# Old keys in units of four pages: 128x2048 VectorE instructions in place of 128x1024

## The chip, the cores and the metric

The kernel runs on one core of a Trainium2 chip. The metric is the time of one execution on the device in microseconds (us); lower is better. The profile is of one execution on that core.

## What is computed

One inference step of a two-layer decoder trunk, for a prompt of 1024 tokens and for 8 samples of one new token each, whose past is 8192 positions long. Layer 0 runs stick-breaking attention beside an RWKV-7 recurrence, layer 1 a gated DeltaNet; each is followed by a convolutional feed-forward network. All is fp32. What matters here is the attention of the samples over their old keys and values, which lie in a pool of pages of 128 positions:

```python
rows = pool[layer, page_table]                       # 64 pages of (128, 8 heads, 64) per sample
z = einsum('bthd,bshd->bhts', q, past_k) * scale + bias
u = log_sigmoid(-z);  after = reverse_cumsum(u) - u
w = exp(log_sigmoid(z) + after)
o = einsum('bhts,bshd->bthd', w, past_v)
```

Per sample that is 64 key pages and 64 value pages of 256 KB each; for 8 samples 512 of each.

## The kernel before, in words

The program is a row of phases with a barrier between them: projections of layer 0 (queries and keys, values, then the RWKV columns in `pb_phase`), prompt attention, the recurrent stage (`rwkv_phase`), output projection, feed-forward, and then layer 1. TensorE has all the projections. The old pages are read beside two of the phases, and the class `Pages` holds their buffers, semaphores and steps.

**A page.** SyncE loads key pages (`load_key_page`, L1019 to L1024): it waits until the slot is free (semaphore `k_used`), reads the page's number from the table, and issues one DMA of 256 KB into a ring of 8 slots (`RING`). The DMAs of a slot count on the slot's own semaphore `k_in`. GpSimd does the same for value pages (`load_values`, L1078), into a ring of their own.

**A unit of keys.** `keys_dve` (L1108 to L1122) waits for its pages, multiplies them with the sample's query, which lies broadcast over all partitions in `pg_q` (L1117, result in `pg_prod`), which frees the slots through `k_used`; then it waits for that multiply and sums over the 64 elements of each head (L1121, result in `pg_z`). The next multiply waits for that sum through `reduced`, since there is one `pg_prod`. A unit is two pages, 128x1024 elements.

**The query.** `load_q` (L1017) loads a sample's query when all 64 pages of the sample before are multiplied. In SyncE's queue it stands behind the first eight key pages of the sample (`load_keys`, L1026 to L1032).

**pb_phase** (L843 to L961) does 14 tiles of 128 columns with two buffers. The pages of sample 0 go along. VectorE's order in a tile: take the rounding rest of the next tile's weights (`rest_weights`, L254), two units of keys (four in each of the last two tiles, which are written out behind the loop), then mix the tile's row with the row before it (L934 to L937), which frees the weight buffer. SyncE's order: weights of an even tile, eight key pages, weights of an odd tile. The weights' DMA waits for the mixing of the tile two before.

**rwkv_phase** (L1367 to L2147) has nine iterations by hand, i = 0 to 8. Iteration i solves chunk pair i of the prompt (two chunks of 64 tokens; `level`, a triangular inverse by doubling, L2010 to L2018), walks the state through pair i - 1 (`state`, L2022 to L2030), prepares pair i + 1 (`gate_ones`, `tanh`, `keys`, `lora_bias`, `sigmoid_ones`, `log_decays`, `modified_keys`, `products`, `bonus`), reads the old values of sample i on TensorE (`values_pe`, L1056), and multiplies the old keys of sample i + 1 on VectorE. The order on VectorE is written out: between the other steps stand calls `more(n)`, each of which takes n units from the sample's list, and `more(NPG)` at the end of the iteration takes what is left. The calls from one bias to the next are: 2 units after `bias_dve`; then softplus, `blocks_t`, `exponents_dve`, `state`, `blocks`; then 1, 1, 1 (after blocks, masked keys, gate), tanh, keys, level 1, then 1, lora bias, 1, `state`, sigmoid, 1, level 2, 2, log decays, 1, centre, 1, level 3, 2, modified keys, 1, normed, 2, level 4, 1, products, 2, outputs, bonus, 2, level 5, and the last 10. In all 32 units, of which 22 before level 5.

The next iteration begins with `bias_dve` (L1130), which needs all 64 pages' scores. From it follow ScalarE's logarithms, the softplus, TensorE's cumulative sums (L1045, L1046), the exponents and the weights `pg_w`, and after these TensorE may begin with the sample's value pages.

Of the kernel before, what the change touches and what calls it, by code (L numbers as in the profile page):

```python
# [17 lines left out]
ALU = mybir.AluOpType  # L18
# [3 lines left out]
P = 128  # L22
# [820 lines left out]
def pb_phase(T):  # L843
# [11 lines left out]
    with ExitStack() as ctx:  # L855
# [61 lines left out]
        def _(dve):  # L917
# [8 lines left out]
            def tile(i, st, j, last=False):  # L926
                if not last:
                    rest(2 * i + j + 1, 1 - j)

                first, units = (RING // 2 * j, RING // 4) if i is not LAST else (0, RING // 2)  # L930
                for n in range(units):
                    pages.keys_dve(dve, 0, i if i is not LAST else LAST + j, first + 2 * n)
                dve.wait_ge(row_in, 6 * i + 3 * j + 3 + 6)
# [32 lines left out]
class Pages:  # L966
# [10 lines left out]
    def __init__(self, T, ctx):  # L977
# [15 lines left out]
        self.qr = self.fold[0:NS, :]  # L993
        self.prod = sb("_prod", [P, 2, D_A])
        self.z = sb("_z", [P, H_A, NPG])
# [112 lines left out]
    def keys_dve(self, dve, b, m, n):  # L1108

        g = self.RING * m + n  # L1110
        if not isinstance(g, int) or g == 0:
            dve.wait_ge(self.q_in, 16 * b + 16)
        for e in range(2):
            dve.wait_ge(self.k_in[n + e], 16 * self.loads * b + 16 * m + 16)

        dve.wait_ge(self.reduced, NPG // 2 * b + self.RING // 2 * m + n // 2 + 1)
        dve.tensor_tensor(self.prod[:, :, :], self.kp[:, n:n + 2, :], self.q[:, :].unsqueeze(1).to_broadcast([P, 2, D_A]),  # L1117
                          ALU.mult).then_inc(self.k_used, 2)
        dve.wait_ge(self.k_used, self.RING + NPG * b + g + 2)
        z = self.z[:, :, g:g + 2] if isinstance(g, int) else self.z[:, :, bass.ds(g, 2)]  # L1120
        dve.tensor_reduce(z.rearrange("p h n -> p n h"), self.prod[:, :, :].rearrange("p n (h d) -> p n h d", h=H_A),  # L1121
                          AX.X, ALU.add).then_inc(self.reduced, 1)  # L1122
# [5 lines left out]
    def bias_dve(self, dve, b):  # L1128
        dve.wait_ge(self.reduced, NPG // 2 * b + NPG // 2 + 1)
        dve.tensor_tensor(self.zb[:, :].rearrange("p (h n) -> p h n", h=H_A), self.z[:, :, :],  # L1130
# [236 lines left out]
def rwkv_phase(T):  # L1367
# [17 lines left out]
    with ExitStack() as ctx:  # L1385
# [526 lines left out]
        def _(dve):  # L1912
# [151 lines left out]
            for i in range(NPAIR + 1):  # L2064
                local, walk, sample = i < NPAIR, i >= 1, i < NS
                units = iter(range(0, NPG, 2))

                def more(n):
                    for _, g in zip(range(n if i + 1 < NS else 0), units):
                        pages.keys_dve(dve, i + 1, g // Pages.RING, g % Pages.RING)  # L2070

# [972 lines left out]
```

## Time and profile before

| | |
|---|---|
| Median of 3 runs | 4905.45 us (4897.6 to 4918.18) |
| The profiled execution's time | 4911.91 us |
| Its span in the profile | 4909.5 us |
| Mean granted TensorE clock | 0.887 |
| PE, DVE, ACT, POOL busy | 4047.4, 2406.4, 1128.4, 384.7 us |
| `pb_phase` | about 245 to 450 us |
| `rwkv_phase` | about 736 to 1830 us; keys until 1628 |
| DVE multiplies of keys (L1117) | x256, 313.2 us busy |
| DVE sums of keys (L1121) | x256, 312.7 us busy |

The profile gives for each engine its busy time, for each instruction its start and length, for each idle time of an engine what ended it, and for each DMA its issue and the time to its landing. PE is TensorE, DVE is VectorE, ACT is ScalarE, POOL is GpSimd, SPq is the queue of SyncE, which issues the key pages' DMAs. A time such as 1096.13 is us from the span's start. Where a helper records the instructions of many steps they have one line: L1914 is such a helper. Engines run their own streams and meet only at semaphores, so a share of busy time alone doesn't say what ends a stage.

### The profile page before, as it was taken

What the parts mean: (1) busy time and instruction counts of PE and PEld (TensorE: products, weight loads), DVE (VectorE), ACT (ScalarE), POOL (GpSimd) and SP (SyncE); (2) the same over time, 40 slices, a digit from 0 to 9 for tenths busy, and PEclk for the clock granted to TensorE, in tenths of its full rate; (3) what the DMA queues carried; (4) which work ended last, traced back from release to release, by engine and by line L of the source; (5) the groups of instructions that cost most, each with busy time, mean ns of one, the idle gap of its engine ahead of it and who ended that gap; (6) DMA issues with size and microseconds to landing.
All of it is one profiled execution on the core that took longest, in us unless ns stands there. A gap on an engine that the chain in (4) does not pass through costs nothing. (4 is left out here: it accounts for less than half of the span.)

```text
span 4909.5 us, 79431 instructions
## 1 busy us (share of the span) xinstructions
PE 4047.4 (82%) x29645; PEld 3363.8 (69%) x29645; DVE 2406.4 (49%) x3151; ACT 1128.4 (23%) x1776; POOL 384.7 (8%) x709
## 2 busy tenths in 40 slices
PE   6786887777777758899989699969899456999999
PEld 6685323333333437899989698857777356999999
DVE  2156878888888432444431244444444343334411
ACT  3211552212122111222220222232222112222300
POOL 0000003222222200000000000000000000000000
PEclk8898998888888859999999899987777578999999
DMA  2153007878788513111112222220110132111122
GB/s 95 69 157 121 26 26 280 280 271 275 272 277 275 180 49 116 52 43 52 43 62 77 86 79 87 86 67 18 36 36 6 46 121 78 46 49 43 47 78 65
DMA packets 214323, 512.08 MB, mean 104 GB/s; under 512 B 32305, under 2 KB 69569, under 8 KB 207546
## 3 DMA queue, kind: packets, MB, share of 16 engines
q1 hardware_dynamic: 155914, 321.58, 20.2%
q0 software_dynamic: 58192, 187.57, 10.7%
q8 instruction: 141, 2.31, 0.2%
q14 instruction: 76, 0.62, 0.0%
HBM read 454.87 MB, written 54.56 MB: 104 GB/s over the span
## 5 line engine op out<-in xcount | busy, mean ns | idle before, releaser
L262 PE MATMUL ps<-ffn_hh,up_wh 128*128 128x344 f32 x2112 | 678.4, 321 | 60.0 <-DVE up_wl L254 60.0
L264 PE MATMUL ps<-ffn_hl,up_wh 128*128 128x344 f32 x2112 | 676.7, 320 | 0.0
L263 PE MATMUL ps<-ffn_hh,up_wl 128*128 128x344 f32 x2112 | 676.0, 320 | 0.0
L262 PEld LDWEIGHTS ps<-ffn_hh,up_wh 128*128 128x128 f32 x2112 | 398.6, 189 | 61.0 <-issue 61.0
L1056 PE MATMUL ps<-pg_v,pg_w 128*8 128x512 f32 x1024 | 343.4, 606 | 78.9 <-DMA pg_v<-in_v_pages 76.3
L263 PEld LDWEIGHTS ps<-ffn_hh,up_wl 128*128 128x128 f32 x2112 | 398.6, 189 | 0.0
L264 PEld LDWEIGHTS ps<-ffn_hl,up_wh 128*128 128x128 f32 x2112 | 398.5, 189 | 0.0
L457 PE MATMUL ps<-down_ah,down_wh 128*128 128x344 f32 x1056 | 343.0, 325 | 31.9 <-DVE down_al L491 18.9
L1117 DVE TENSOR_TENSOR pg_prod<-pg_k,pg_q 128x1024 f32<-128x1024 f32 x256 | 313.2, 1224 | 71.7 <-DMA pg_q<-scratch_pg_q 25.5
L458 PE MATMUL ps<-down_ah,down_wl 128*128 128x344 f32 x1056 | 339.9, 322 | 0.0
L459 PE MATMUL ps<-down_al,down_wh 128*128 128x344 f32 x1056 | 339.9, 322 | 0.0
L1078 POOL DMA_DIRECT2D pg_v<-in_v_pages x512 | 277.3, 542 | 665.5 <-PE ps L1056 451.6
L1121 DVE TENSOR_REDUCE pg_z<-pg_prod 128x16 f32<-128x1024 f32 (+1 forms) x256 | 312.7, 1221 | 11.4 <-DVE pg_prod L1117 0.2
L262 PE MATMUL ps<-hh,odd_wh 128*128 128x344 f32 x792 | 258.3, 326 | 63.4 <-DVE odd_wl L254 63.4
L1056 PEld LDWEIGHTS ps<-pg_v,pg_w 128*8 128x8 f32 x1024 | 43.0, 98 | 328.6 <-DMA pg_v<-in_v_pages 299.1
L264 PE MATMUL ps<-hl,odd_wh 128*128 128x344 f32 x792 | 254.8, 322 | 0.0
L263 PE MATMUL ps<-hh,odd_wl 128*128 128x344 f32 x792 | 254.7, 322 | 0.0
L457 PEld LDWEIGHTS ps<-down_ah,down_wh 128*128 128x128 f32 x1056 | 200.6, 190 | 36.5 <-issue 30.1
L458 PEld LDWEIGHTS ps<-down_ah,down_wl 128*128 128x128 f32 x1056 | 201.4, 191 | 0.0
L459 PEld LDWEIGHTS ps<-down_al,down_wh 128*128 128x128 f32 x1056 | 200.7, 190 | 0.0
L262 PEld LDWEIGHTS ps<-hh,odd_wh 128*128 128x128 f32 x792 | 150.4, 190 | 72.0 <-ACT odd_row L2207 41.8
L254 DVE TENSOR_TENSOR down_wl<-down_w,down_wh 128x896 fp32r<-128x896 f32 (+1 forms) x48 | 54.4, 1136 | 280.8 <-ACT down_wh L249 280.8
(410 smaller groups left out, 7368.0 us busy)
## 6 DMA issues: line engine op xcount, KB each, us to landing
pg_k<-in_k_pages SPq DMA_DIRECT2D x512, 256.0 KB, 4.8
pg_v<-in_v_pages POOLq DMA_DIRECT2D x512, 256.0 KB, 5.0
up_w<-in_w_ff SPq DMA_DIRECT2D x44, 1034.0 KB, 4.8
odd_w<-in_w_odd SPq DMA_DIRECT2D x33, 526.0 KB, 4.0
scratch_odd_rows<-odd_cv POOLq DMA_DIRECT2D x32, 516.0 KB, 4.5
down_w<-in_w_down SPq DMA_DIRECT2D x32, 448.0 KB, 3.4
dn_x<-scratch_odd_rows SPq DMA_DIRECT2D x8, 1536.0 KB, 8.2
scratch_x<-out_x POOLq DMA_DIRECT2D x16, 516.0 KB, 3.0
```

What stands on the lines that cost most here:

```text
L254: dve.tensor_tensor(lo, w, hi.bitcast(F32), ALU.subtract).then_inc(rest_ready, 1)
L262: pe.matmul(out, wh, xh, start=(k == 0), stop=False)
L263: pe.matmul(out, wl, xh, start=False, stop=False)
L264: mm = pe.matmul(out, wh, xl, start=False, stop=(k == n - 1))
L457: pe.matmul(out, hi, ah[:, k, g[c]], start=(k == 0), stop=False)
L458: pe.matmul(out, lo, ah[:, k, g[c]], start=False, stop=False)
L459: mm = pe.matmul(out, hi, al[k][:, g[c]], start=False, stop=(k == FT - 1))
L1056: pe.matmul(self.T.ps[c:c + H_A, 7, :], wts[:, :, g], self.vp[:, n, :], start=(g < 4), stop=(g >= NPG - 4), tile_position=(0, c), skip_gro ...
L1078: pool.dma_start(self.vp[:, g % self.RING, :], self.T.io["v_pages"][bass.ds(page, 1), :, :] .rearrange("a p n -> (a p) n")).then_inc(self. ...
L1117: dve.tensor_tensor(self.prod[:, :, :], self.kp[:, n:n + 2, :], self.q[:, :].unsqueeze(1).to_broadcast([P, 2, D_A]), ALU.mult).then_inc(se ...
L1121: dve.tensor_reduce(z.rearrange("p h n -> p n h"), self.prod[:, :, :].rearrange("p n (h d) -> p n h d", h=H_A), AX.X, ALU.add).then_inc(se ...
```

## The change

A unit becomes four pages. `keys_dve` waits for four slots' DMAs, multiplies 128x2048 elements in one instruction, frees four slots with it, and sums 128x2048 elements in the next. `pg_prod` has four page places in place of two. The counts on `reduced` follow. In the tile loop of `pb_phase` there is one unit where there were two (two where there were four at the end). In `rwkv_phase` `more(n)` still counts in steps of two pages: it raises a target by 2n pages and issues a unit whenever four pages are due. So the units stand after `bias_dve` (4 pages due), after the masked keys (8), level 1 (12), the sigmoid (16), level 2 (20), centre (24), after level 3 (28), normed (34, unit 28 to 31), level 4 (36), products (40), bonus (44), and five at the end. The ring keeps its eight slots, and the loads and their order stay as they are.

```diff
@@ pb_phase, VectorE
-                first, units = (RING // 2 * j, RING // 4) if i is not LAST else (0, RING // 2)
+                first, units = (RING // 2 * j, RING // 8) if i is not LAST else (0, RING // 4)
                 for n in range(units):
-                    pages.keys_dve(dve, 0, i if i is not LAST else LAST + j, first + 2 * n)
+                    pages.keys_dve(dve, 0, i if i is not LAST else LAST + j, first + 4 * n)
@@ Pages.__init__
-        self.prod = sb("_prod", [P, 2, D_A])
+        self.prod = sb("_prod", [P, 4, D_A])
@@ Pages.keys_dve
-        for e in range(2):
+        for e in range(4):
             dve.wait_ge(self.k_in[n + e], 16 * self.loads * b + 16 * m + 16)
 
-        dve.wait_ge(self.reduced, NPG // 2 * b + self.RING // 2 * m + n // 2 + 1)
-        dve.tensor_tensor(self.prod[:, :, :], self.kp[:, n:n + 2, :], self.q[:, :].unsqueeze(1).to_broadcast([P, 2, D_A]),
-                          ALU.mult).then_inc(self.k_used, 2)
-        dve.wait_ge(self.k_used, self.RING + NPG * b + g + 2)
-        z = self.z[:, :, g:g + 2] if isinstance(g, int) else self.z[:, :, bass.ds(g, 2)]
+        dve.wait_ge(self.reduced, NPG // 4 * b + self.RING // 4 * m + n // 4 + 1)
+        dve.tensor_tensor(self.prod[:, :, :], self.kp[:, n:n + 4, :], self.q[:, :].unsqueeze(1).to_broadcast([P, 4, D_A]),
+                          ALU.mult).then_inc(self.k_used, 4)
+        dve.wait_ge(self.k_used, self.RING + NPG * b + g + 4)
+        z = self.z[:, :, g:g + 4] if isinstance(g, int) else self.z[:, :, bass.ds(g, 4)]
@@ Pages.bias_dve
-        dve.wait_ge(self.reduced, NPG // 2 * b + NPG // 2 + 1)
+        dve.wait_ge(self.reduced, NPG // 4 * b + NPG // 4 + 1)
@@ rwkv_phase, VectorE
-                units = iter(range(0, NPG, 2))
+                at = [0, 0]
 
                 def more(n):
-                    for _, g in zip(range(n if i + 1 < NS else 0), units):
-                        pages.keys_dve(dve, i + 1, g // Pages.RING, g % Pages.RING)
+                    at[1] = min(at[1] + 2 * n, NPG)
+                    while i + 1 < NS and at[0] + 4 <= at[1]:
+                        pages.keys_dve(dve, i + 1, at[0] // Pages.RING, at[0] % Pages.RING)
+                        at[0] += 4
```

## Rows read from the trace of the kernel before

**Rows 1.** Busy time by stretch, recurrent stage: stretch, length, engines, clock, DMA share, GB/s
```profile
1108.00:1236.00 128.00, 97.30 (x1007) 49.35 (x1006) 111.14 (x116) 27.04 (x51) 36.59 (x66) 0.86 0.82 279
```

**Rows 2.** Waits of VectorE, 736 to 1632 us: total us, times, longest
```profile
DVE pg_prod L1117 <- DMA pg_q<-scratch_pg_q: 25.5, 6, 4.4
...
DVE pg_prod L1117 <- DMA pg_k<-in_k_pages: 2.0, 3, 1.3
```

**Rows 3.** Waits of TensorE, 736 to 1632 us
```profile
PE ps L1574 <- ACT rw_mr L1802: 89.6, 7, 16.3
```

**Rows 4.** Timeline of VectorE, one sample: start, length, instruction, idle before
```profile
995.67 0.69 DVE L1130 TENSOR_TENSOR pg_zb<-pg_z,vecs_sb 128x512 f32<-128x512 f32 x1
...
1024.08 0.36 DVE L1919 TENSOR_SCALAR rw_eg<-rw_eg 128x256 f32<-128x256 f32 x1
...
1035.81 0.87 DVE L1914 TENSOR_TENSOR rw_dh<-rw_Hx,ps 64x256 f32<-64x256 f32 x2 [0.16 <-PE ps L1596]
...
1056.17 0.72 DVE L2014 COPY_PREDICATED rw_mxm<-consts,ps 128x512 f32<-128x512 int32 x1
...
1096.13 1.23 DVE L1117 TENSOR_TENSOR pg_prod<-pg_k,pg_q 128x1024 f32<-128x1024 f32 x1 [0.31 <-DVE rw_mxt L2017]
1097.39 1.22 DVE L1121 TENSOR_REDUCE pg_z<-pg_prod 128x16 f32<-128x1024 f32 x1
...
1119.66 1.22 DVE L1117 TENSOR_TENSOR pg_prod<-pg_k,pg_q 128x1024 f32<-128x1024 f32 x1
...
1122.17 0.69 DVE L1130 TENSOR_TENSOR pg_zb<-pg_z,vecs_sb 128x512 f32<-128x512 f32 x1
```

**Rows 5.** Timeline of SyncE's queue: first start, length until the last's end
```profile
1098.18 25.14 SPq L1023 DMA_DIRECT2D pg_k<-in_k_pages  x20
1123.50 0.33 SPq L1017 DMA_DIRECT2D pg_q<-scratch_pg_q  x1
...
1102.02 2.17 SPq L1023 DMA_DIRECT2D pg_k<-in_k_pages  x2
```

**Rows 6.** Waits of SyncE's queue, 1095 to 1124 us
```profile
SPq L1022 <- DVE pg_prod L1117: 1.1, 2, 1.0
```

**Rows 7.** Timeline of VectorE in the projection stage, one tile
```profile
326.00 1.22 DVE L1117 TENSOR_TENSOR pg_prod<-pg_k,pg_q 128x1024 f32<-128x1024 f32 x1
...
331.20 1.22 DVE L934 TENSOR_TENSOR pb_xs<-pb_row 128x1024 f32<-128x1024 f32 x1
...
332.53 1.29 DVE L937 SCALAR_TENSOR_TENSOR pb_xs<-pb_xs,pb_w,pb_row 128x1032 f32<-128x1032 f32 x1
339.34 1.23 DVE L254 TENSOR_TENSOR pb_wl<-pb_w,pb_wh 128x1024 fp32r<-128x1024 f32 x1 [5.52 <-ACT pb_wh L249]
```

**Rows 8.** Waits of TensorE, 245 to 430 us
```profile
PE ps L262 <- DVE pb_wl L254: 28.1, 12, 4.0
```

**Rows 9.** Instructions of the tile pg_k: ns min/median/max, first and last start
```profile
L1117 DVE TENSOR_TENSOR pg_prod<-pg_k,pg_q x256: 1204/1225/1236, 250.8 to 1625.4; 128x1024 f32<-128x1024 f32 x128
L1914 DVE TENSOR_TENSOR pg_k<-pg_k,rw_kv x3: 2291/2292/2293, 1783.1 to 1800.6; 128x2048 f32<-128x2048 f32 x3
...
L2134 DVE TENSOR_REDUCE rw_sa<-pg_k x1: 3569/3569/3569, 1785.4 to 1785.4; 128x32 f32<-128x2048 f32 x1
```

**Rows 10.** Timeline of ScalarE, 1021 to 1026 us
```profile
1025.14 0.29 ACT L1743 ACTIVATE rw_sg<-rw_eg 128x128 f32<-128x128 f32 x1
```

**Rows 11.** Timeline of TensorE: the last products before level 3
```profile
1052.85 1.10 PE L1537 MATMUL ps<-rw_mxt,rw_my 64*64 64x64 f32 x32
```

**Rows 12.** Timeline of GpSimd: one value page
```profile
1085.61 0.54 POOL L1078 DMA_DIRECT2D pg_v<-in_v_pages  x1 [0.62 <-issue]
```

**Rows 13.** DMA issues, KB each, median us to landing: 1085:1125, 1100:1110, 1112:1124
```profile
pg_k<-in_k_pages SPq DMA_DIRECT2D x27, 256.0 KB, 5.3
...
pg_k<-in_k_pages SPq DMA_DIRECT2D x7, 256.0 KB, 6.1
...
pg_k<-in_k_pages SPq DMA_DIRECT2D x9, 256.0 KB, 3.4
```

## The prediction

> **What bounds the kernel now.** The change touches old keys alone, so I read first where those 512 pages are multiplied: in the stage that projects the RWKV columns (245 to 450 us; 64 pages, sample 0) and in the recurrent stage (736 to 1632 us; 448 pages, samples 1 to 7). A "unit" is one multiply and its sum.
>
> The busy times by stretch say that in the recurrent stage VectorE is the busiest engine, with 111.1 of 128 us in a stretch of one sample's length, while the DMA engines stand at 0.82 and move 279 GB/s [rows 1]. The reader should see two things near a limit, not one. The waits say what VectorE stops for: 4.2 us a sample for the query's DMA (25.5 in six times), key pages hardly ever (2.0 us in all) [rows 2]; the rest of its idle time is in gaps between dependent instructions and waits under 3 us. TensorE waits 89.6 us for a ScalarE copy, behind VectorE's work [rows 3]: TensorE has room. So a sample takes what VectorE's instructions take plus the query wait: bias at 995.67, bias again at 1122.17, period 126.5 us [rows 4]. In the last 26 us of it, from 1096.13, ten units stand back to back, 2.61 us apart (nine steps in 23.53 us) [rows 4].
>
> Then the queue that feeds them. In that same tail SyncE issues 20 key pages in 25.14 us, 1.26 us each, and waits 1.1 us for free slots in all [rows 5, 6]: VectorE takes a page per 1.31 us, SyncE can issue one per 1.26. The key stream is as close to its limit as VectorE. This is what the sum hangs on.
>
> In the projection stage VectorE's timeline shows a loop of 14.5 us a tile: two units (from 326.00), three mixing instructions (331.20 to 332.53 + 1.29), 5.5 us idle for the next tile's rounded weights, their split (339.34, some 1.15 us until the next unit), again [rows 7]. The weights' DMA waits for that mixing. TensorE waits for the split 28.1 us in 12 times, 2.3 us each [rows 8]. So here the units lie on the path.
>
> **What one unit costs.** A 128x2048 multiply stands in the trace at 2.292 us, one of 128x1024 at 1.225 us [rows 9]: 0.158 us saved where two become one. A contiguous sum over 128x2048 isn't there. The 128x1024 one takes 1.22 us, as its multiply does, so I take 1.22 + (2.292 - 1.225) = 2.29 us; bounds: that, and twice 1.22 = 2.44 us. (The 3.57 us of the 128x2048 sum in rows 9 reads across rows of the tile; this one reads along them as before, so it isn't a bound.) With the gaps of 0.03 and 0.14 us of rows 4, a unit of four pages steps 2.29 + 0.03 + 2.29 + 0.14 = 4.75 us against 2 x 2.61 = 5.23: 0.48 us saved. There are 16 such per sample: 7.7 us a sample, 54 us for seven. If that were all, the answer would be easy; the parts follow.
>
> **Part 1, projection stage.** From the first unit's start to the mixing's first subtraction is 5.20 us (326.00 to 331.20) [rows 7]; with one unit 2.29 + 0.14 + 2.22 = 4.65. Saved 0.55 us on the loop in 12 tiles = 6.6 us, and in the last two tiles (four units each, two after) 0.95 us each = 1.9. SyncE: all four slots of a half are now freed at once, 2.3 us after the unit's start; its four issues at 1.26 us end 2.3 + 4 x 1.26 = 7.3 us after it, or 7.8 with a turn of its loop, and the mixing ends 4.65 + 2.6 = 7.3 us after it, so the odd tile's weights, which stand behind those issues, may leave up to 0.5 us late. I keep 8.5 us of gain; bounds 0 and 8.5. TensorE's slack of 2.3 us covers 0.55.
>
> **Part 2, recurrent stage, per sample, from bias to bias.**
> (a) The first four pages: one unit for two, -0.5 us, in front of everything.
> (b) From there to the second state update. Units now start only when four pages are due: none before the masked keys, none between the gate's "plus one" and the tanh. VectorE then meets waits that units covered: the tanh needs ScalarE's result, 1.35 us after the gate's instruction began (1024.08, then 1025.14 + 0.29) [rows 4, 10]; and the state update already waits for TensorE, 0.16 us at 1035.81 [rows 4]. It cannot start earlier, since TensorE's part follows the start of the stretch and not the units. VectorE arrives there 1.5 to 2 us early and idles. It has done 12 pages there instead of 14. The saving in this stretch is lost and two pages are postponed.
> (c) From there to the last level of the solve: 15 units before (15 x 2.48 + 5 x 0.14 = 37.9 us), 8 after (8 x 4.61 = 36.9), and two gaps of some 0.15 us fewer: -1.2 us. The levels before have slack: TensorE ends level 3 at 1053.95, VectorE takes it at 1056.17 [rows 4, 11]. The value pages, which TensorE takes in between, come as before: GpSimd issues one per 1.16 us, by its own pace (0.54 us and 0.62 of issue) [rows 12].
> (d) The tail: five units for ten. Before 26.04 us (1096.13 to 1122.17). VectorE alone needs 5 x 4.61 + 4 x 0.14 = 23.6. But the ring has eight pages, so now it is two halves, each freed at once when a multiply ends, and reloaded by four issues in a row. From the end of a multiply the first issue takes 0.8 us (1096.13 + 1.23 to 1098.18), three more take 3.8, the loop's turn 0.5 for one half (two issues over it span 2.17, so 2.17 - 0.33 = 1.84 apart instead of 1.26) [rows 4, 5]: the last page is issued 4.6 to 5.0 us later and lands after L. VectorE is back at that half 2.29 + 0.17 + 4.75 = 7.2 us after the multiply's end. It waits when L is over about 2.4 us. L is 5.3 us (median of this stretch), 6.1 at its fullest, 3.4 once the values have stopped [rows 13]. Walking the five units with 5.3 for the first two reloads and 3.4 for the rest, from the first unit's start: starts at 0, 7.0 (waited 2.3), 12.2 (0.4), 17.7 (0.8), 22.5 (0), end 27.1. That is +1.1 us against 26.04, not -2.4. With one L throughout the tail takes about 18.4 + 2L.
> (e) The query: its DMA stands behind the eight pages of the next sample, of which the last multiply now frees four, not two. Before: multiply ends 1119.66 + 1.22, query issued 1123.50, 2.6 us [rows 4, 5]; now 0.8 + 4 x 1.26 = 5.1 with the issue. That is 2.5 later; the last sum is 1.07 us longer; so the wait at the query grows by 1.4 us, six times.
> Sum: 7 x (-0.5 - 1.2 + 1.1) + 6 x 1.4 = -4.2 + 8.4 = +4.2 us. With part 1: -4.3 us. Six semaphore counts change and cost nothing. The product buffer grows by 4 KB per partition and moves no work.
>
> The profiled execution took 4911.9 us (span 4909.5), which gives 4907.6; it lies 6.5 above the median, so for the median 4905.45 I forecast 4901.
>
> **The tiling rule.** The rows give each VectorE instruction a fixed part of 0.158 us whatever its size [rows 9]. The Trainium skill ("VectorE: DVE Perf Modes", the section on the TRN2 errata) says that one large tile pays the latency once and many small ones pay it each time, so tile large. By that alone this change gains everything; that is the first rival. **The landing.** A page takes 3.4 us to land in the quiet and 5.3 beside the values [rows 13]. The Trainium skill ("DMA: Bandwidth & Descriptors", the cost table after the chain of events) gives 2.0 us plus bytes over 436 GB/s, 2.6 us for a page: by it the tail would take 23.6 us and the time would be some 25 us lower; the trace disagrees.
>
> **Rivals.**
> A. All of VectorE's saving arrives: 54 + 8.5 = 62 us, 4843. For it: the tail is pure VectorE. Against: SyncE idles 1.1 us in 25. Chance 0.07.
> B. Pages land at 3 us in the tail, and the tail falls to 18.4 + 6 = 24.4 us: (-1.7 - 1.6) x 7 + 8.4 - 8.5 = -23; with the query hardly later, 4875 to 4882. For it: bursts are further apart. Against: the DMA engines are full there. 0.12.
> C. The projection stage gives nothing, since the burst of key issues holds its weights back: 4910. 0.15.
> D. Slower: the half ring starves VectorE in the tail because four pages at a time land later than single pairs. Price: at L = 7 the tail takes 32.4 us, +6.3 per sample, 7 x 4.6 + 8.4 - 8.5 = +32, 4937. It decides from L = 6.5 on. For it: 6.1 already occurs. Against: as many bytes in more time. 0.10.
> E. The change does less than it says: if the wide sum costs 2.44 us, 16 x 0.15 x 7 = 17 us come back where VectorE isn't waiting: 4918 at most. 0.06.
> The forecast itself has 0.50. A measurement of this kernel tells 0.5%, 24.5 us, from no change. Faster by more: A, most of B: 0.17. Slower: D, 0.10. Same: 0.73. The range reaches from rival B to just short of D, with E and C inside: 4875 to 4928.
>
> **What would show it.** 128 multiplies of 128x2048 near 2.29 us and 128 sums near 2.29; VectorE busy time lower by 128 x 0.31 = 40 us; waits for key pages in the recurrent stage up from 2.0 to some 25 us; the query wait from 25.5 to some 34; the wait at 1035.81 from 0.2 to some 1.5 us a sample, and a new one at the tanh; a period near 126.5 us; a loop of 13.9 us in the projection stage. Wrong: if the key waits stay near 2 us, the ring's argument falls, and the time goes to B; if the period passes 130 us, to D.

## The result, and the profile after

The changed kernel takes 4932.29 us (median of 5 runs, 4920.85 to 4948.9) against 4905.45: the ratio is 1.0058, interval 1.0034 to 1.0083. It is slower by 27 us. The forecast was 4901 and the range ended at 4928, so both missed; the side was that of rival D, to which the prediction gave 0.10.

The arithmetic went as it was costed. These are lines of the page of the kernel after: span, busy time by engine, and the two instructions of a unit.

```profile
span 4930.7 us, 79017 instructions
...
PE 4047.3 (82%) x29645; PEld 3358.7 (68%) x29645; DVE 2369.8 (48%) x2895; ACT 1128.3 (23%) x1776; POOL 383.3 (8%) x709
...
L1117 DVE TENSOR_TENSOR pg_prod<-pg_k,pg_q 128x2048 f32<-128x2048 f32 x128 | 293.3, 2291 | 115.1 <-DMA pg_k<-in_k_pages 55.0
...
L1121 DVE TENSOR_REDUCE pg_z<-pg_prod 128x32 f32<-128x2048 f32 (+1 forms) x128 | 292.8, 2288 | 5.6 <-DVE pg_prod L1117 0.2
```

A multiply takes 2.291 us, a sum 2.288, as forecast; VectorE is busy 2369.8 us where it was busy 2406.4. VectorE works 37 us less, and the kernel takes 27 us more. The answer stands in the same rows, in the third column of the multiply: 115.1 us idle ahead of it, 55.0 of them with a key page as what came last. A stretch of one sample's length (compare [rows 1]) and the waits of VectorE from 730 to 1660 us (compare [rows 2]; columns: total us, times, longest) say it by name.

```profile
1127.00:1256.00 129.00, 93.36 (x952) 45.46 (x952) 104.22 (x83) 25.93 (x48) 35.60 (x65) 0.87 0.80 269
```

```profile
DVE pg_prod L1117 <- DMA pg_k<-in_k_pages: 48.2, 30, 4.0
DVE pg_prod L1117 <- DMA pg_q<-scratch_pg_q: 35.1, 6, 6.1
DVE rw_dh L1914 <- PE ps L1596: 22.9, 12, 3.7
...
DVE rw_th L1924 <- ACT rw_sg L1743: 8.2, 8, 1.0
```

VectorE is still the busiest engine of the stretch, but no longer the bound for all of it. Key pages cost 48.2 us where they cost 2.0, the query 35.1 where it cost 25.5. The bias came every 124.55 us on average before (756.14 to 1627.96, seven periods) and comes every 129.38 us now (750.13 to 1655.77): 33.8 us in all, more than the whole loss. Over the six samples that also wait for a query, the period was 126.40 us and is 131.36: past the 130 us that the prediction named as the sign of rival D.

The timeline of VectorE in the same sample as [rows 4] shows where in the sample they lie.

```profile
996.56 0.69 DVE L1130 TENSOR_TENSOR pg_zb<-pg_z,vecs_sb 128x512 f32<-128x512 f32 x1
1003.20 2.29 DVE L1117 TENSOR_TENSOR pg_prod<-pg_k,pg_q 128x2048 f32<-128x2048 f32 x1 [5.95 <-DMA pg_q<-scratch_pg_q]
...
1027.87 0.22 DVE L1924 TENSOR_SCALAR rw_th<-rw_th 64x128 f32<-64x128 f32 x1 [1.02 <-ACT rw_sg L1743]
...
1038.57 0.87 DVE L1914 TENSOR_TENSOR rw_dh<-rw_Hx,ps 64x256 f32<-64x256 f32 x2 [1.96 <-PE ps L1596]
...
1098.33 2.29 DVE L1117 TENSOR_TENSOR pg_prod<-pg_k,pg_q 128x2048 f32<-128x2048 f32 x1 [0.41 <-DVE rw_mxt L2017]
...
1105.34 2.29 DVE L1117 TENSOR_TENSOR pg_prod<-pg_k,pg_q 128x2048 f32<-128x2048 f32 x1 [2.40 <-DMA pg_k<-in_k_pages]
...
1112.27 2.29 DVE L1117 TENSOR_TENSOR pg_prod<-pg_k,pg_q 128x2048 f32<-128x2048 f32 x1 [2.32 <-DMA pg_k<-in_k_pages]
...
1117.89 2.29 DVE L1117 TENSOR_TENSOR pg_prod<-pg_k,pg_q 128x2048 f32<-128x2048 f32 x1 [1.02 <-DMA pg_k<-in_k_pages]
...
1127.29 0.69 DVE L1130 TENSOR_TENSOR pg_zb<-pg_z,vecs_sb 128x512 f32<-128x512 f32 x1
```

Four places are to be seen. The first unit starts 6.64 us after the bias, for the query. The tanh and the second state update (1027.87, 1038.57) now have waits ahead of them that units used to cover. Then nothing waits for long until 1098.33. The tail, five units that would take 23.6 us by themselves, takes 28.96 (before: 26.04), with 2.3 and 2.2 us lost ahead of its second and its third unit and 0.9 ahead of the fourth.

What the pages do in that tail: the issues of SyncE's queue (start, length until the last's end), and their landings (median us) when asked for each batch of four in turn.

```profile
1095.90 4.06 SPq L1023 DMA_DIRECT2D pg_k<-in_k_pages  x4
...
1101.44 4.04 SPq L1023 DMA_DIRECT2D pg_k<-in_k_pages  x4
...
1130.20 0.33 SPq L1017 DMA_DIRECT2D pg_q<-scratch_pg_q  x1
```

```profile
pg_k<-in_k_pages SPq DMA_DIRECT2D x4, 256.0 KB, 5.1
...
pg_k<-in_k_pages SPq DMA_DIRECT2D x4, 256.0 KB, 5.8
...
pg_k<-in_k_pages SPq DMA_DIRECT2D x4, 256.0 KB, 5.7
rw_xs<-scratch_xs_rows POOLq DMA_DIRECT2D x1, 896.0 KB, 8.2
...
pg_k<-in_k_pages SPq DMA_DIRECT2D x4, 256.0 KB, 3.0
```

The multiply that frees the half ends at 1098.33 + 2.29 = 1100.62. The four reloads are issued from 1101.44, the last at 1105.15, and VectorE can use that half at 1112.27: 11.6 us after it was freed. Its own work on the other half takes 7.2 us; delayed itself at 1105.34, it came back after 9.3. The columns of the next view are as in [rows 1], one line for each step of the tail, the last for two.

```profile
1098.33:1105.34 7.01, 4.15 (x18) 1.50 (x17) 4.58 (x3) 2.43 (x5) 3.30 (x7) 0.99 0.93 336
1105.34:1112.27 6.93, 6.63 (x68) 5.02 (x66) 4.58 (x3) 2.99 (x7) 1.49 (x2) 0.76 1.03 369
1112.27:1117.89 5.62, 0.00 (x0) 0.00 (x0) 4.57 (x2) 0.00 (x0) 0.00 (x0) 0.78 0.88 285
1117.89:1127.29 9.40, 0.00 (x0) 0.00 (x0) 9.16 (x5) 0.00 (x0) 0.00 (x0) 0.50 0.62 193
```

While the DMA engines stand at 0.93 and 1.03, the unit waits 2.3 us; when GpSimd's stream has ended they fall to 0.88, where it waits 0.9 us, and then to 0.62, where it doesn't wait. The Trainium skill ("DMA: Bandwidth & Descriptors", the cost table after the chain of events) gives, for a transfer issued from GpSimd, a fixed 2.0 us and the bytes over 436 GB/s; applied to a page, which SyncE issues, that is an estimate of 2.6 us. Only the 3.0 us of the batch issued when GpSimd's stream had ended comes near it; beside another stream the runs show twice that.

In the projection stage the last mixing ends up where it was, at 449.9 us instead of 450.3. Two tiles of its timeline, to be read beside [rows 7], and SyncE's queue in them:

```profile
326.81 2.28 DVE L1117 TENSOR_TENSOR pg_prod<-pg_k,pg_q 128x2048 f32<-128x2048 f32 x1
331.44 1.21 DVE L934 TENSOR_TENSOR pb_xs<-pb_row 128x1024 f32<-128x1024 f32 x1
332.77 1.29 DVE L937 SCALAR_TENSOR_TENSOR pb_xs<-pb_xs,pb_w,pb_row 128x1032 f32<-128x1032 f32 x1
340.61 1.23 DVE L254 TENSOR_TENSOR pb_wl<-pb_w,pb_wh 128x1024 fp32r<-128x1024 f32 x1 [6.54 <-ACT pb_wh L249]
...
347.70 1.30 DVE L937 SCALAR_TENSOR_TENSOR pb_xs<-pb_xs,pb_w,pb_row 128x1032 f32<-128x1032 f32 x1
354.28 1.23 DVE L254 TENSOR_TENSOR pb_wl<-pb_w,pb_wh 128x1024 fp32r<-128x1024 f32 x1 [5.29 <-ACT pb_wh L249]
```

```profile
322.03 11.92 SPq L1023 DMA_DIRECT2D pg_k<-in_k_pages  x8
334.23 15.28 SPq L865 DMA_DIRECT2D pb_w<-in_w_pb  x2
```

From the unit to the mixing's subtraction it is 4.63 us, as predicted (4.65). But the odd tile's weights, issued at 334.23 right behind eight key pages, are split only at 340.61, 6.4 us later; the even tile's at 354.28, 5.1 us after their issue at 349.18. The idle time is 6.54 against 5.29, and the tiles alternate: over the stage the mixing comes after 13.5 to 13.9 us and then after 14.3 to 16.3. The split waits for ScalarE's rounding, and that for the weights: the trace has their DMA landing 3.8 to 4.2 us after its issue in the even tiles and 4.7 to 6.6 in the odd ones. In the kernel before it is 3.7 to 4.4 in all tiles.

### The profile page after: what moved, and what is told of

Same layout as the page of the kernel before. It is cut to its first block and busy times, and to the rows that moved or that the text cites. A ratio compares the mean times of both kernels' runs of the same rounds, so it can differ in the third digit from the quotient of the medians.

```text
span 4930.7 us, 79017 instructions
## 1 busy us (share of the span) xinstructions
PE 4047.3 (82%) x29645; PEld 3358.7 (68%) x29645; DVE 2369.8 (48%) x2895; ACT 1128.3 (23%) x1776; POOL 383.3 (8%) x709
## 5 line engine op out<-in xcount | busy, mean ns | idle before, releaser
L1056 PE MATMUL ps<-pg_v,pg_w 128*8 128x512 f32 x1024 | 355.4, 605 | 71.4 <-DMA pg_v<-in_v_pages 68.7
L1117 DVE TENSOR_TENSOR pg_prod<-pg_k,pg_q 128x2048 f32<-128x2048 f32 x128 | 293.3, 2291 | 115.1 <-DMA pg_k<-in_k_pages 55.0
L1121 DVE TENSOR_REDUCE pg_z<-pg_prod 128x32 f32<-128x2048 f32 (+1 forms) x128 | 292.8, 2288 | 5.6 <-DVE pg_prod L1117 0.2
```

What stands on the lines that cost most here:

```text
L1056: pe.matmul(self.T.ps[c:c + H_A, 7, :], wts[:, :, g], self.vp[:, n, :], start=(g < 4), stop=(g >= NPG - 4), tile_position=(0, c), skip_gro ...
L1117: dve.tensor_tensor(self.prod[:, :, :], self.kp[:, n:n + 4, :], self.q[:, :].unsqueeze(1).to_broadcast([P, 4, D_A]), ALU.mult).then_inc(se ...
```

## The experiments

Each ran on the same chip as a fresh series of the kernel before. e1 to e4 share one (4908.52 us, 29 runs), e5 to e8 another (4904.44, 18), e9 to e11 a third (4907.92, 17). "Key waits" and "query waits" are those of VectorE in the recurrent stage; "tail" is from the first unit behind the last level of the solve to the next bias.

**e1: the query ahead of the last four key pages.**

```
@@ load_keys
-        for n in range(self.RING):
+        for n in range(self.RING // 2):
             self.load_key_page(sp, b, 0, n)
         self.load_q(sp, b)
+        for n in range(self.RING // 2, self.RING):
+            self.load_key_page(sp, b, 0, n)
```

> The changed kernel, but SyncE issues the query's DMA after the first four key pages of the next sample, not after eight. Theory (half ring): the query was late because four page issues of 1.26 us, all freed by the last multiply, stood before it. Its wait falls from 35.1 us in six times (5.9 each) to some 12 to 16 (2.5 less or a little more each, to about 2 to 2.7), the period by some 3 us per sample, and the time to about 4915 (-17). The waits for key pages (48.2 us) stay, within 5 us. Rival (the key stream's total rate bounds the sample, wherever the query stands): the query's wait falls, the key waits grow by the same amount, and the time stays at 4932 +- 8.

Measured: 4905.83 us, ratio 1.0003 (0.9991 to 1.0014). Its waits:

```profile
DVE pg_prod L1119 <- DMA pg_k<-in_k_pages: 52.3, 30, 3.8
...
DVE pg_prod L1119 <- DMA pg_q<-scratch_pg_q: 7.1, 6, 1.6
```

The first unit comes 1.3 to 2.3 us after the bias, no longer 6.0 to 6.8, and the bias period falls to 125.12 us. The key waits stay. The query's place in the queue takes away 28 of the 35 us of waits for it, and 26 us of time: the wait at the query is on the path, as the prediction took it. As much as the whole change lost can be had back without touching the ring; the ring's own loss is still there.

**e2: the last 20 pages of a sample in ten pairs.**

```
@@ keys_dve, with the width w as a parameter; in the recurrent stage
-                    while i + 1 < NS and at[0] + 4 <= at[1]:
-                        pages.keys_dve(dve, i + 1, at[0] // Pages.RING, at[0] % Pages.RING)
-                        at[0] += 4
+                    while i + 1 < NS:
+                        w = 4 if at[0] < Pages.TAIL else 2
+                        if at[0] + w > at[1]:
+                            break
+                        unit = pages.units(i + 1) + min(at[0], Pages.TAIL) // 4 + max(at[0] - Pages.TAIL, 0) // 2
+                        pages.keys_dve(dve, i + 1, at[0] // Pages.RING, at[0] % Pages.RING, w, unit)
+                        at[0] += w
@@ TAIL = 44
```

> The changed kernel, but the last 20 pages of each sample are taken in ten units of two pages, as before the change; the 44 pages before stay in units of four. Theory (half ring): the tail goes back from 29 us to 26 us or a little more (the last four-page unit before it still frees four slots at once, which costs up to 2 us once), the waits for keys in the recurrent stage fall from 48 to under 20 us, the query's from 35 to some 26. Time 4932 - 7 x 2.5 - 6 x 1.5 = 4905, that is, level with the kernel before. Rival (the loss lies in the middle, in the later units and the waits they lay bare): the tail gets shorter, but under 10 us come back: 4922 or more.

Measured: 4912.76 us, ratio 1.0015 (1.0006 to 1.0024), 20 us under the kernel after. Key waits 17.6 us, query waits 24.5, tails of 26.9 to 28.6 us where they were 27.6 to 31.3. The half ring in the tail is the cause of about 30 us of key waits and of the query's extra 10; but the time came back by less than that. The pairs themselves cost VectorE 11 us (2381.0 us busy for 2369.8), and part of the rest shows in a place that the edit doesn't touch. The stretch behind the bias, 20 us and 20 us, of samples 1 and 3 of this kernel:

```profile
864.10:884.10 20.00, 11.34 (x156) 8.16 (x156) 12.06 (x16) 4.73 (x10) 0.00 (x0) 0.67 0.32 103
884.10:904.10 20.00, 18.94 (x300) 13.04 (x302) 15.88 (x16) 5.23 (x10) 5.38 (x10) 1.00 0.56 181
1118.20:1138.20 20.00, 12.19 (x88) 8.55 (x90) 10.28 (x10) 4.59 (x9) 0.00 (x0) 0.50 0.33 102
1138.20:1158.20 20.00, 19.46 (x316) 14.81 (x316) 16.22 (x16) 4.32 (x9) 4.32 (x8) 0.86 0.45 142
```

The granted clock is 0.67 and then full in sample 1; in sample 3 it is at the lower level (0.50, 1.2 GHz) for the first 20 us and at 0.86 in the next, and the first level of the solve is taken 32.4 us after the bias instead of 29.2. It is 32.2 to 32.4 in samples 3 to 6, some 3 us each.

**e3: page numbers fixed.** The page's number is no longer read from the table, so SyncE's issue is shorter. This kernel leaves out the lookup: it reads the pool's pages in order, which are other old keys than the table's.

```
@@ load_key_page
-        page = sp.value_load(self.table[0:1, bass.ds(g, 1)], min_val=0, max_val=self.T.n_phys - 1)
-        sp.dma_start(self.kp[:, n, :], self.T.io["k_pages"][bass.ds(page, 1), :, :].rearrange("a p n -> (a p) n"))\
+        sp.dma_start(self.kp[:, n, :], self.T.io["k_pages"][bass.ds(g, 1), :, :].rearrange("a p n -> (a p) n"))\
```

> The changed kernel, but key pages are read from the pool in order of their number and not by the page table, so SyncE needs no table load and no page number: the transfers, their sizes and the ring stay the same, only SyncE's time per page falls. Left out: the lookup (the old keys are other pages of the pool). Theory (half ring, its reload is issue plus landing): at some 0.5 us per page in place of 1.26 the last of four pages is issued 2.3 us earlier, the waits for keys fall from 48 us to under 15, the query's by 2 us or more each to under 25 in all, and the time to 4932 - 30 to - 45, about 4895. Rival (the DMA engines' rate bounds the tail, landing takes what the bytes take): landings grow as issues come closer, key waits stay above 35 us, the time at 4920 or more.

Measured: 4905.8 us, ratio 0.9999 (0.9987 to 1.001). Four issues of a half take 2.08 us in place of 4.0. The waits, and the landing of a key page over 900 to 1600 us (median):

```profile
DVE pg_prod L1116 <- DMA pg_k<-in_k_pages: 30.0, 20, 2.8
DVE pg_prod L1116 <- DMA pg_q<-scratch_pg_q: 22.5, 6, 3.9
```

```profile
pg_k<-in_k_pages SPq DMA_DIRECT2D x355, 256.0 KB, 5.3
```

The key waits fall by 18 us, not to nothing: pages issued closer together land later (5.3 us against 5.0 in the kernel after). What SyncE's pace gives, the landing takes back in part. That the pages are now neighbours in the pool could matter too; e9 keeps them as they were. The projection stage gained too: every tile takes 13.5 to 14.0 us and the last mixing starts at 441.1 us. The burst of issues ahead of the odd weights is over sooner there; e4 tests that place by itself.

**e4: in the projection stage, the odd tile's weights between the two halves of the eight key pages.**

```
@@ keys, weights
-            def keys(m):
-                for n in range(RING):
+            def keys(m, half=(0, 1)):
+                for n in range(RING // 2 * half[0], RING // 2 * (half[-1] + 1)):
                     pages.load_key_page(sp, 0, m, n)
...
                 weights(i, 0)
-                keys(i)
+                keys(i, (0,))
                 weights(i, 1)
+                keys(i, (1,))
```

> The changed kernel, but in the projection stage SyncE issues the odd tile's weights between the first four and the last four key pages of the iteration, not behind all eight. Theory (the burst of four pages just ahead of the weights holds up their landing, which ate this stage's gain): the odd tiles' split comes 5.1 to 5.4 us after the weights' issue, as the even ones' does, not 5.8 to 7.7; mixing to mixing is 13.7 to 13.9 us in all tiles of the loop (14.3 before the change); the stage's last mixing starts at some 441 us, against 449.9, and the time falls by 8 us. Rival (TensorE is the bound of the stage once the units are cheaper): the odd tiles' waits move to TensorE's product, and the stage ends within 3 us of 449.9.

Measured: 4926.1 us, ratio 1.005 (1.003 to 1.007). The splits of its weights:

```profile
320.64 1.23 DVE L254 TENSOR_TENSOR pb_wl<-pb_w,pb_wh 128x1024 fp32r<-128x1024 f32 x1 [5.08 <-ACT pb_wh L249]
...
334.06 1.23 DVE L254 TENSOR_TENSOR pb_wl<-pb_w,pb_wh 128x1024 fp32r<-128x1024 f32 x1 [5.02 <-ACT pb_wh L249]
```

Every tile takes 13.4 to 13.8 us, the idle time ahead of the split no longer alternates, and the last mixing comes 10.6 us earlier than in the kernel after (439.3 against 449.9). In the second profile of the kernel after (e11) it came at 445.5, against which e4 is 6.2 us earlier; the median fell by 6 us as well, which 4 and 5 runs with a spread of some 20 us don't show by themselves. The 8.5 us that the prediction gave this stage were there (439.3 against 450.3 and 449.2 in the two profiles of the kernel before), and a queue order withheld most of them.

**e5 and e11: the kernel before and the kernel after once more**, unchanged, for a second profile of each.

> The kernel before, profiled once more, for the spread of the trace's stages. Theory (the changed kernel's prompt attention, 4 us shorter, and its last 130 us of the recurrent stage, 11 us shorter, are no effects of the change but spread between executions): from the last bias to the samples' first sum this profile shows another figure than the 157.4 us of the first, 146 to 157, and the key period stays within 1 us of 124.6 on the mean of seven. Rival (the change shortens them): 157 us again, within 1, and the same attention.

> The changed kernel, profiled once more, for the spread. Theory: key period 129.4 us on the mean of seven within 1.2, of which the samples with TensorE's granted clock at the lower level until 22 us after the bias are 2 to 3 us longer than the others; the tail 27.6 to 31 us. Rival (the longer periods at the end of the stage, 131 to 135 us, come from the keys of those samples and recur in the same samples whatever the clock).

Measured: 4907.35 and 4927.7 us. Key waits 3.7 and 50.7 us, query waits 23.6 and 35.7, mean period 124.85 and 129.51 us, projection stage until 449.2 and 445.5. What the theory rests on repeats. Other stretches move by some 5 us between profiles without regard to the change: from the last mixing to the start of the recurrent stage it is 286.0, 283.1 and 280.7 us in three profiles with pairs (before, e5, e6), and 280.4, 280.6 and 284.9 in three with four pages (after, e11, e1). The longest periods move as well: sample 6 in the kernel after (134.7 us), samples 1 and 5 in e11 (132.7 and 135.8; its other samples with a query wait 128.4 to 130.3). They are the samples with the lower granted clock behind the bias (0.50 over 20 us), so they don't belong to certain samples' keys.

**e6: the kernel before, its query ahead of the last two key pages.**

```
@@ load_keys, against the kernel before
-        for n in range(self.RING):
+        for n in range(self.RING - 2):
             self.load_key_page(sp, b, 0, n)
         self.load_q(sp, b)
+        for n in range(self.RING - 2, self.RING):
+            self.load_key_page(sp, b, 0, n)
```

> The kernel before, with pairs, but SyncE issues the query's DMA after six key pages of the next sample, ahead of the two that the last multiply frees. Theory (the query's DMA is late for the issues ahead of it, in pairs as in fours): the first unit starts some 2.4 us after the bias in place of 4.9, 6 times, so 15 us less: about 4892. Rival (the wait only moves, to keys or to TensorE's sums): the query's wait falls from 25.5 to some 10 us and the time by less than 5.

Measured: 4895.73 us, ratio 0.9982 (0.997 to 0.9995). Query waits 13.1 us instead of the 25.5 of [rows 2]; 12.4 us less wait made 9 us (2 to 15 by the interval). Here too most of the wait is paid, though less than the 15 us that were expected.

**e7: units issued as soon as two of their four pages are due**, so that units stand again ahead of the tanh and the second state update.

```
@@ recurrent stage
-                    while i + 1 < NS and at[0] + 4 <= at[1]:
+                    while i + 1 < NS and at[0] + 2 <= at[1]:
```

> The changed kernel, but a unit of four is issued as soon as two of its pages are due, so units stand also between the gate and the tanh and before the second state update. Theory (part of the loss in the middle comes from waits that no unit covers): the wait at the tanh falls from 8.2 us in all to under 2, that of the state update from 22.9 to about 10 to 14, the second level is taken 2 us earlier or more relative to the bias (48.5 now), and the time falls by 7 x 1 to 7 x 2.5, to 4915 to 4925. Rival (only the tail counts, since the key stream is what ends a sample): these waits fall, the key waits (48 us) grow by as much, time 4932 +- 6.

Measured: 4928.2 us, ratio 1.0049 (1.0032 to 1.0066), within the spread of the kernel after. The waits at the tanh are gone and those at the state update are 18.2 us for 22.9, together 12.9 us less. But a wait stands in their place that the kernel after doesn't have, for TensorE's products ahead of a level of the solve:

```profile
DVE rw_mxm L2014 <- PE ps L1537: 12.6, 9, 4.2
```

So the waits were moved and not removed, and from the first unit to the tail it takes 93.5 us in samples 0 to 5, for 93.8. The tails are now 28.7 to 31.4 us (29.95 on average for 29.14) with 50.8 us of key waits in all, 2.6 more. The time is the rival's, but not for its reason, since the key waits didn't grow by what the others lost. What the waits in the middle cost isn't told by this run.

**e8: four pages a unit in the projection stage only, with e4's order; the recurrent stage in pairs, with e6's query.** It is built on the kernel after: e4's diff, e6's place for the query (behind six pages), and e2's width parameter with TAIL = 0, which makes the recurrent stage that of the kernel before.

> Units of four pages in the projection stage alone, with the odd tile's weights issued between the key pages' halves; units of two pages in the recurrent stage, and the query's DMA after six pages. Theory: the projection stage gives its 10 us (last mixing at some 440 us), the query its 15, and the recurrent stage keeps the period of the kernel before less 2.4 us: about 4881, faster than both kernels. Rival (what is gained ahead of a phase or at the query is lost again at the next wait): 4895 or more.

Measured: 4888.04 us, ratio 0.9967 (0.9955 to 0.9979): 8 us under e6, and the last mixing starts at 441.4 us for e6's 448.4. So the wide units pay where the ring isn't the limit and the weights don't stand behind them.

**e9: SyncE reads the four page numbers of a half ahead of its waits, then issues four transfers.**

```
+    def load_key_half(self, sp, b, m, h):
+        g0, half = NPG * b + self.RING * m + self.RING // 2 * h, self.RING // 2
+        ids = [sp.value_load(self.table[0:1, bass.ds(g0 + e, 1)], min_val=0, max_val=self.T.n_phys - 1) for e in range(half)]
+        for e, page in enumerate(ids):
+            n = half * h + e
+            sp.wait_ge(self.k_used, g0 + e + 1)
+            sp.dma_start(self.kp[:, n, :], self.T.io["k_pages"][bass.ds(page, 1), :, :].rearrange("a p n -> (a p) n"))\
+              .then_inc(self.k_in[n], 16)
@@ load_keys
-        for n in range(self.RING):
-            self.load_key_page(sp, b, 0, n)
+        self.load_key_half(sp, b, 0, 0)
+        self.load_key_half(sp, b, 0, 1)
         self.load_q(sp, b)
         with sp.Fori(1, self.loads) as m:
-            for n in range(self.RING):
-                self.load_key_page(sp, b, m, n)
+            self.load_key_half(sp, b, m, 0)
+            self.load_key_half(sp, b, m, 1)
```

> The changed kernel, but in the recurrent stage SyncE reads the page numbers of a half (four) before it waits for its slots, and then issues the four DMAs one after the other: the same pages, the right result, and the four issues of a freed half in some 2 us instead of 4.5. With fixed page numbers the key waits had fallen from 48 to 30 us, not under 15, since the last of four landed up to 8.8 us after its issue: the closer the issues, the longer the landing. Theory (now: reload is issue plus landing, and the landing is in part the bytes of the four pages themselves beside the values): as with fixed numbers, key waits 25 to 35 us, query wait 20 to 27 us in all, time 4905 to 4918. Rival (it was the missing table load as such, or another order of pages in memory, that helped there): key waits stay over 42 us and the time over 4922.

Measured: 4907.9 us, ratio 1.0003 (0.999 to 1.0017). Four issues behind a freed half, and the waits:

```profile
1126.10 1.97 SPq L1032 DMA_DIRECT2D pg_k<-in_k_pages  x4
```

```profile
DVE pg_prod L1126 <- DMA pg_k<-in_k_pages: 33.7, 19, 3.5
DVE pg_prod L1126 <- DMA pg_q<-scratch_pg_q: 22.0, 6, 3.8
```

24 us come back from SyncE's queue alone: the four issues take 2.0 us instead of 4.0, the tail 28.05 us on average instead of 29.14, and the query is issued sooner as well. Landings grow here too (median 5.5 us over 1160 to 1560), and 33.7 us of key waits stay.

**e10: four pages a unit everywhere, with e9's read-ahead, e4's order and e1's query.**

> Units of four everywhere, with the three remedies together: page numbers read ahead per half, the query's DMA after four pages, the odd tile's weights between the halves in the projection stage. Theory (the three losses are separate and add up): 4932 - 26 (query, as measured) - 7 (weights) - 10 to - 15 (reading ahead) = 4884 to 4890. Rival (they overlap, since the ring's reload bounds the sample once the query is early): 4898 or more.

Measured: 4884.11 us, ratio 0.9942 (0.9928 to 0.9956), the fastest of all. Waits:

```profile
DVE pg_prod L1127 <- DMA pg_k<-in_k_pages: 36.1, 21, 3.2
```

The query's waits are 1.7 us; the keys' are as in e9. With the queue put in order the change comes out ahead of the kernel before by 24 us, as its theory had it (4884 to 4890), and of e8, which leaves the recurrent stage in pairs, by some 7 (both against their own series: 23.8 and 16.4 us; the two intervals just overlap). The 24 us aren't all the merge's: e6 gave pairs 9 us by the query's place alone, and pairs with the numbers read ahead were not run.

## Why the prediction was wrong, point by point

Unit cost: right, 4.75 us a unit in the tail (1117.89 to 1122.64). Right too that the ring and not VectorE's arithmetic decides, and the four places where time would be lost. The sizes were not.

**Part 1, the projection stage: the first step that failed.** It kept 8.5 us and allowed for odd weights leaving "up to 0.5 us late". They do leave at once, 0.17 us after the mixing ends (332.77 + 1.29 to 334.23). They land late: 6.4 us from issue to split against 5.1, 4.7 to 6.6 us from issue to landing against 3.8 to 4.2. The gain was 0.4 us in this profile, 3.7 between e5 and e11. Rival C had this outcome, with the burst of key issues as its reason; e4 shows the reason by issuing four of those pages behind the weights. It was the weights' landing beside the pages just issued, not their own issue, that came late. Cost of the step: 5 to 8 us.

**(d), the tail: the step that weighs most.** The walk took L, the landing of a page, as 5.3, 5.3 and 3.4 us and found waits of 2.3, 0.4, 0.8 and 0. Measured in this sample: 2.3, 2.2, 0.9 and 0. The second is the one that failed: the half freed at 1100.62 had its last page issued at 1105.15, as the walk had it (4.5 us after the multiply's end), and was ready at 1112.27, so L was 7 us and not 5.3. The DMA engines stand at 0.93 and 1.03 there, with value pages and the next sample's rows (896 KB) in flight. The third wait came out right by accident: its batch too landed in 5.7 us and not in 3.4, but the unit ahead of it was as late. The mistake was to read L as the median over a stretch, and to let it fall as soon as the values stop, where VectorE waits for the last page of a batch. The plainer formula that the prediction gave beside the walk, 18.4 + 2L, makes 29.0 us at L = 5.3. On average the tail takes 29.14 us (27.6 to 31.3) against 26.27 before: +2.9 where the prediction had +1.1, over seven samples 12 us more. e2, e3 and e9 show that the reload of a half is what costs: taking the tail in pairs, or issuing the four faster, cut the key waits from 48.2 to 17.6, 30.0 and 33.7 us. No run made the ring deeper.

Rival D had this mechanism and priced it from L = 6.5 on. That limit held only while part 1's 8.5 us and the middle's 12 us stood in the sum on the other side. Without them L = 5.3, the median that the prediction had in its rows, is enough: 7 x 2.9 + 9.6 = 30 us.

**(e), the query: nearly right.** +1.4 us six times; measured 1.6 (35.1 - 25.5 = 9.6 us in six). The sum as printed, 0.8 + 4 x 1.26, makes 5.8 us and not 5.1; the 5.1 that it went on with is what the trace has, 5.3 (the last multiply ends at 1124.93, the query is issued at 1130.20). e1 and e6 show that it was on the path.

**(a) to (c), the middle: too hopeful by about 1.5 us a sample.** From the first unit to the last level it takes 93.9 us in samples 1 to 5, against 94.1 before; the prediction had -1.7 (its own terms in (c) add up to -1.3 and not -1.2). The waits it named are there (8.2 us at the tanh; 1.96 us at 1038.57 in this sample, for 1.5 to 2 predicted). One reason of the rest fits what the trace has: "six semaphore counts change and cost nothing" left out that a unit now waits for four pages' semaphores and not two. Ahead of a unit behind another instruction VectorE idles 0.41 us (1098.33) where it idled 0.31 ([rows 4], 1096.13). At eight or nine places a sample that is 0.8 us. No run separates the two more waits from the wider instruction. The prediction added the middle's and the tail's terms as if VectorE carried both. Whether a unit done sooner in the middle only meets the stream of pages sooner in the tail isn't shown: e7 took the waits at the tanh away and met TensorE's products instead.

**The sum.** The prediction had +4.2 us for the recurrent stage, the trace has +33.8: of the missing 29.6 the tail is 12.4, the middle of samples 0 to 5 (up to the tail's first unit) 10.5, the query 1.2, and the middle of sample 6 another 5.5, of which some 2.5 go with TensorE's clock (below). The projection stage's 0.4 in place of 8.5 makes 8 more. That would be 38 us over the forecast; the profiles differ by 21.2 where the forecast had -4.3, 25.5 us over. What went the other way: 5.6 us ahead of the stage, which e5, e6, e1 and e11 show to be the spread of that stretch, and 10.8 us between the last bias and the first of the two sums near the stage's end (L2134) (157.4 to 146.6 us; in e5 and e11 151.9 to 145.2; with four pages in e1 151.3), less 4 us behind it. No unit stands in that stretch; the granted clock in its first two 10 us is 0.50 and 0.50 before, and 0.54 and 0.83 after. Whether part of it belongs to the change stays open.

**Chances.** The prediction knew that SyncE's 1.26 us a page and VectorE's 1.31 us stood level. A change that makes the consumer take twice as much at once, on a stream without reserve and with a ring of two such portions, should have had "slower" as its likeliest case, not 0.10.

## What to carry to other kernels

Before instructions are merged into larger ones, look at what they free and when: a ring that is two portions deep has to be reloaded, issue by issue and landing included, within the one portion that is left. Count that loop (here 0.8 us + four issues + the landing of the last page, 11.6 us, against 7.2 us of work) with the landing beside everything else in flight, and for the last of the batch, not the median. And see what stands behind the batch in the same queue: a small transfer that others wait for (the query, the odd weights) goes ahead of it; the query's place was worth 26 us here, and the weights' place some 6 to 10 us of the projection stage. With both and the page numbers read ahead, the kernel with the merge that lost 27 us stands 24 us under the kernel before. Some 7 of these separate it from the kernel that is in pairs in the recurrent stage (e8), which has no read-ahead; what the merge is worth there against pairs with the same queue no run tells. Nor was the plain remedy tried, a ring of more than two portions.

## What the runs showed of the hardware that was not expected

TensorE's granted clock behind the bias isn't the same in every sample. These are 20 us behind the bias of samples 5 and 6 of the kernel after, and the 20 us that follow, and in the timeline of VectorE the first state update of each.

```profile
1389.58:1410.00 20.42, 10.40 (x100) 7.12 (x102) 10.31 (x11) 4.58 (x9) 0.00 (x0) 0.58 0.41 115
1410.00:1430.00 20.00, 19.61 (x329) 14.65 (x326) 16.39 (x16) 5.02 (x10) 5.28 (x10) 0.94 0.52 162
1521.09:1541.00 19.91, 9.75 (x70) 6.59 (x72) 10.27 (x10) 4.26 (x8) 0.00 (x0) 0.50 0.40 117
1541.00:1561.00 20.00, 19.03 (x264) 14.44 (x261) 13.78 (x15) 4.04 (x10) 3.23 (x6) 0.80 0.33 108
```

```profile
1409.95 0.87 DVE L1914 TENSOR_TENSOR rw_dh<-rw_Hx,ps 64x256 f32<-64x256 f32 x2 [1.33 <-PE ps L1596]
...
1543.96 0.87 DVE L1914 TENSOR_TENSOR rw_dh<-rw_Hx,ps 64x256 f32<-64x256 f32 x2 [3.70 <-PE ps L1596]
```

TensorE comes out of the end of a tail, where the view above shows it without work (0.00 from 1112.27 on), and starts at the lower level (1.2 GHz). In sample 5 it is back near 2.4 GHz in the second line (0.94), in sample 6 later (0.80), and the state update comes 22.87 us after the bias for 20.37: 2.5 us for the same work. The lower level over the first 20 us is seen in four of the seven samples of e2, in two each of e3 and e11. It isn't the change's: in e5, the kernel before, sample 1 has it too (0.50; the state update after 20.99 us, in the other samples with a query wait after 18.7 to 19.2). No run here tells what decides it.

Second, a page's landing goes with how closely its neighbours are issued: a median of 5.0 us over 900 to 1600 us where four issues take 4 us, 5.3 and 5.5 where they take 2 (e3, e9). It is the last page of a half that pays, and VectorE waits for that one: its median is 5.4 us in the kernel after, 6.3 in e3 and 6.6 in e9, that of the first page 4.5, 4.6 and 4.8. From the first issue of a half until all four pages are there it takes 9.2 us, 8.2 and 8.2: half of the 2 us saved on the issues comes through.
